# Attention of a two-block kernel: P turned in 32x32 blocks, P·V on row quarters, the output product in two halves

## What is computed

```python
qkv = h @ w_qkv                                   # 2048 x 2560: 2048 q, 256 k, 256 v
q, k = rope(rms_norm(q)), rope(rms_norm(k))       # per head of 64
scores = q . k / 8, only keys j with  i - 128 < j <= i
m = max(scores, sink);  p = exp(scores - m)
probs = p / (sum(p) + exp(sink - m))
out = probs @ v                                   # 256 x 2048
x = x + out @ w_o                                 # w_o is 2048 x 2048
x = x + (silu(h2 @ w_gate) * (h2 @ w_up)) @ w_down   # h2 = rms_norm(x)
```

## Time and profile before

| | |
|---|---|
| median of 3 runs | 1928.45 us |
| the profiled execution | 1928.84 us, span of the program in it 1927.0 us |
| PE (TensorE matmul) busy | 1920.7 us, 100% of the span |
| DVE (VectorE), ACT (ScalarE), POOL (GpSimd) busy | 1302.3, 1076.2, 556.6 us |
| granted TensorE clock | full in all 40 slices |
| DMA | 352 MB, 183 GB/s over the span, engines 50 to 90% busy |

### The profile page before, as it was taken

How to read it: one execution, slowest core, us unless ns; L and a number is a source line. 1 busy time by engine, 2 the same in 40 slices (tenths; PEclk the granted TensorE clock), 3 DMA queues, 4 the chain that set the end, 5 groups by cost and what they waited for, 6 DMA issues and landing times.

```text
span 1927.0 us, 26536 instructions
## 1 busy us (share of the span) xinstructions
PE 1920.7 (100%) x9696; PEld 1576.4 (82%) x9696; DVE 1302.3 (68%) x1852; ACT 1076.2 (56%) x1405; POOL 556.6 (29%) x616
## 2 busy tenths in 40 slices
PE   9999999999999999999999999999999999999999
PEld 7888878888888888888887778888888888888887
DVE  5899967546878888887667877555555555544443
ACT  7444466547768696875557775544444444443332
POOL 1899853306060413302401106022222222220000
PEclk9999999999999999999999999999999999999999
DMA  9665656566555555555564445666666666666664
GB/s 322 190 194 178 186 164 198 174 209 184 160 162 164 157 169 160 167 156 180 186 197 141 123 141 189 193 196 192 191 195 186 196 195 195 190 192 196 193 193 161
DMA packets 183152, 352.47 MB, mean 183 GB/s; under 512 B 11792, under 2 KB 12304, under 8 KB 183056
## 3 DMA queue, kind: packets, MB, share of 16 engines
q1 hardware_dynamic: 182912, 351.20, 59.7%
q10 hardware_dynamic: 144, 0.01, 0.0%
HBM read 349.07 MB, written 2.10 MB: 182 GB/s over the span
## 4 chain that ended last, share of the span: by engine, by line
PE 89%; DVE 3%; ACT 3%; POOL 2%; issue 1%; DVEq 1%; POOLq 0%; DMA 0%; ACTq 0%; SPq 0%
PE acc L550 28%; PE acc L552 28%; PE acc L551 28%; POOL kb L467 1%; PE T L660 1%; POOL kf L467 1%; DVEq L1175 1%; ACT E L1002 1%; PE T L509 1%; DVE w_lo L1189 1%; PE T L755 1%; PE T L744 1%; ACT w_hi L797 1%; DVE E L1416 0%; PE T L732 0%
## 5 line engine op out<-in xcount | busy, mean ns | idle before, releaser
L1189 DVE TENSOR_TENSOR w_lo<-raw,w_hi 128x1024 fp32r<-128x1024 f32 x568 | 699.1, 1234 | 533.9 <-ACT w_hi L797 526.1
L797 ACT ACTIVATE w_hi<-raw 128x1024 fp32r<-128x1024 f32 x656 | 688.7, 1057 | 594.7 <-PE acc L552 576.0
L550 PE MATMUL acc<-w_hi,h_hi 128*128 128x512 f32 x1884 | 741.7, 394 | 0.4 <-DVE w_lo L1189 0.2
L552 PE MATMUL acc<-w_hi,h_lo 128*128 128x512 f32 x1884 | 733.7, 389 | 0.0
L551 PE MATMUL acc<-w_lo,h_hi 128*128 128x512 f32 x1884 | 733.6, 389 | 0.0
L550 PEld LDWEIGHTS acc<-w_hi,h_hi 128*128 128x128 f32 x1884 | 353.7, 188 | 80.0 <-issue 5.1
L552 PEld LDWEIGHTS acc<-w_hi,h_lo 128*128 128x128 f32 x1884 | 353.6, 188 | 74.0
L551 PEld LDWEIGHTS acc<-w_lo,h_hi 128*128 128x128 f32 x1884 | 353.9, 188 | 71.2
L498 POOL COPY fT<-fq 32x256 f32<-32x256 f32 x176 | 110.9, 630 | 388.1 <-DVE fq L1651 381.3
L436 POOL TENSOR_TENSOR w_lo<-raw,w_hi 128x1024 fp32r<-128x1024 f32 x80 | 190.4, 2409 | 71.5 <-ACT w_hi L797 71.4
L1269 DVE SCALAR_TENSOR_TENSOR T<-vpad,feat,T 128x256 f32<-128x256 f32 x464 | 182.4, 476 | 0.0
(11 more groups left out here) (245 smaller groups left out, 1581.7 us busy)
## 6 DMA issues: line engine op xcount, KB each, us to landing
raw<-in_hgrn_w_in_dram SPq DMA_DIRECT2D x160, 512.0 KB, 3.7
raw<-in_conv_w_in_dram SPq DMA_DIRECT2D x96, 512.0 KB, 4.1
raw<-in_ffn_w_gate_dram SPq DMA_DIRECT2D x88, 512.0 KB, 4.4
raw<-in_ffn_w_up_dram SPq DMA_DIRECT2D x88, 512.0 KB, 4.2
raw<-in_ffn_w_down_dram SPq DMA_DIRECT2D x88, 512.0 KB, 4.8
raw<-in_attn_w_qkv_dram SPq DMA_DIRECT2D x40, 512.0 KB, 4.0
raw<-in_conv_w_out_dram SPq DMA_DIRECT2D x32, 512.0 KB, 4.6
raw<-in_hgrn_w_out_dram SPq DMA_DIRECT2D x32, 512.0 KB, 4.6
```

Source lines behind the costliest of these rows:

```text
L550: nc.tensor.matmul(o, hi[:, kt, a], w_hi[:, slot, kk, :], start=kt == 0, stop=False)
L552: last = nc.tensor.matmul(o, lo[:, kt, a], w_hi[:, slot, kk, :], start=False, stop=kt == p.chunks * CK - 1)
L797: A(w_hi[:, slot, :, :], raw[:, slot, :, :], ACT.Copy).then_inc(hi_ready, 1)
L1189: TT(w_lo[:, slot, :, :], raw[:, slot, :, :], rounded(w_hi[:, slot, :, :]), ALU.subtract).then_inc(split_ready, 1)
```

## The change

1. `low_by_pool`: GpSimd makes `w_lo` of three chunks in eight (i mod 8 = 7, 0, 1) in place of two.
2. P is no longer turned on TensorE. VectorE turns it in 32x32 blocks (`p_turn`, one instruction a head), which leaves block b of the keys of query quarter a on partitions 32a to 32a+31. `mix_v` now runs once a group, behind chunk e+16 (e+14 for g = 3): 60 matmuls of 32 rows by 64 columns by 128 streamed columns, each of the four row quarters into its own PSUM bank, two column halves side by side. V is spread to the four row quarters by GpSimd (`v_rows`), `PT` now holds eight heads and shares its place with `kvtok`.
3. `scale_p` moves from VectorE to GpSimd, two instructions for a pair of heads; VectorE keeps the reciprocal (`inverse`).
4. `y_out_hi` (ScalarE, e+20; e+18 for g = 3) and `y_low` (VectorE, e+21; e+18) take a whole group, four instructions each, 256 strided columns.
5. `att_out` becomes eight segments of four chunks: the four column groups over channels of heads 0 to 15, then again over the others. VectorE adds the first parts to `x` (`first_part`), four more times two additions. The interleaved start is gone.
6. Of x, two column groups (2 and 3) are turned on TensorE at the end of `att_out`, not one.

```diff
-    return 24 <= i < 50 and i % 8 < 2
+    return 23 <= i < 50 and i % 8 in (7, 0, 1)
...
+    def segment(self, k):
+        return k + self.columns if self.in_parts else k
+    def row(self, k, c):
+        return self.chunks * (k // self.columns) + c if self.in_parts else c
+    def first_reads(self, k):
+        return k == 0 or self.in_parts and k == self.columns
...
-            ... ("att_out", 1, 4, {"lead": 2}),
+            ... ("att_out", 1, 8, {"chunks": CPG // 2}),
...
+            def v_rows():
+                pool.wait_ge(a_ev, 1)
+                pool.wait_ge(a_T, 1)
+                for a in range(4):
+                    for b in range(4):
+                        nc.gpsimd.tensor_copy(vrows[a * QUARTER:(a + 1) * QUARTER, b::4, :], kvtok[b * QUARTER:(b + 1) * QUARTER, :, KVH * HD:])
+                nc.gpsimd.drain().then_inc(a_rows, 1)
+
+            def scale_p(g, i):
+                pool.wait_ge(a_inv, 4 * g + i + 1)
+                for tb in range(TB):
+                    p, inv = sm[:, 2 * i:2 * i + 2, (1 + tb) * P:2 * (1 + tb) * P], ast[:, 6, 8 * tb + 2 * i:8 * tb + 2 * i + 2]
+                    last = nc.gpsimd.tensor_tensor(p, p, inv.unsqueeze(2).to_broadcast([P, 2, (1 + tb) * P]), ALU.mult)
+                last.then_inc(a_n, 1)
...
+                    i = n - ph["kv_q"].chunk0
+                    if i % 8 == 1:
+                        for p in range(4):
+                            scale_p(i // 8 - 3, p)
...
-                    if need is not None and k == 0:
-                        need(c)
+                    row = p.row(k, c)
+                    if need is not None and p.first_reads(k):
+                        need(row)
...
             def q_turn(g):
                 pe.wait_ge(a_rp, g + 2)
                 pe.wait_ge(a_cp, 2)
                 if g:
-                    pe.wait_ge(a_ptc, 8 * g)
+                    pe.wait_ge(a_sm, 8 * g)
+                if g > 1:
+                    pe.wait_ge(a_lo, 4 * (g - 1))
                 transposes(T01, ar, a_T)
...
-            def turn_p(g, i):
-                ...
-                    for b in range(3):
-                        last = nc.tensor.transpose(T[:, h % 2, b * P:(b + 1) * P], sm[:, h, (b + 1) * P:(b + 2) * P], ident[:, :])
-            def mix_v(g, i):
-                ...
+            def mix_v(g):
+                pe.wait_ge(a_rows, 1)
+                pe.wait_ge(a_pt, 4 * g + 4)
+                pe.wait_ge(a_sm, 8 * (min(g + 1, 3) + 1))
+                if g:
+                    pe.wait_ge(a_lo, 4 * g)
                 for tb in range(TB):
+                    for step in range(5):
+                        for a in range(4):
+                            blocks = range(4 + a, 4 + a + 5) if tb else range(a + 1)
+                            if step >= len(blocks):
+                                continue
+                            b, r = blocks[step], slice(a * QUARTER, (a + 1) * QUARTER)
+                            key = b if b < 4 else b - 4
+                            for c in range(2):
+                                o = T[c * HD:(c + 1) * HD, a, :].rearrange("p (i t q) -> p i t q", t=TB, q=QUARTER)[:, 0:4, tb, :]
+                                w = PT[r, c:8:2, b * QUARTER:(b + 1) * QUARTER]
+                                last = nc.tensor.matmul(o, vrows[r, key, g * HD:(g + 1) * HD], w, start=step == 0, stop=step == len(blocks) - 1)
                 last.then_inc(a_o, 1)
...
-                for i in range(4):
-                    at.put(e + 8 + i, lambda g=g, i=i: turn_p(g, i))
-                    at.put(e + 9 + i, lambda g=g, i=i: mix_v(g, i))
+                at.put(e + 16 if g < 3 else e + 14, lambda g=g: mix_v(g))
...
-            stream("att_out", 0, y_hi, hy_lo, early, lambda c: pe.wait_ge(a_lo, c + 1))
+            stream("att_out", 0, y_hi, hy_lo, at.later(40).with_(last_x), lambda c: pe.wait_ge(a_lo, 2 * (c + 1)))
...
-            def p_copy(g, i):
-                ...
+            def y_out_hi(g):
+                act.wait_ge(a_o, g + 1)
+                for i in range(4):
+                    A(by_quarters(y_hi, 4 * g + i), mixed(i).rearrange("p a (b i) -> p a b i", b=TB), ACT.Copy).then_inc(a_hi, 1)
...
+                    at.put(e + 20 if g < 3 else e + 18, lambda g=g: y_out_hi(g))
...
+            def first_part(name, k):
+                dve.wait_ge(chunk_used, ph[name].done(0, k))
+                for tb in range(TB):
                     TT(x[:, tb, group_columns(k)], acc[:, ph[name].pair(k), tb, :], x[:, tb, group_columns(k)],
                        ALU.add).then_inc(pair_free[ph[name].pair(k)], 1)
...
+            def inverse(g, i):
                 dve.wait_ge(a_p, 4 * g + i + 1)
                 l, inv = ...
-                V.reciprocal(inv, l)
+                V.reciprocal(inv, l).then_inc(a_inv, 1)
+            def p_turn(g, i):
+                dve.wait_ge(a_n, 4 * g + i + 1)
+                ...
+                for h in (2 * i, 2 * i + 1):
+                    last = V.transpose(PT[:, h, :], sm[:, h, P:4 * P])
+                last.then_inc(a_pt, 1)
+            def y_low(g):
+                dve.wait_ge(a_hi, 4 * g + 4)
+                for i in range(4):
+                    low(by_quarters(hy_lo, 4 * g + i), mixed(i).rearrange("p a (b i) -> p a b i", b=TB), by_quarters(y_hi, 4 * g + i), a_lo)
...
+                    for i in range(4):
+                        at.put(e + 11 + i, lambda g=g, i=i: p_turn(g, i))
+                    at.put(e + 21 if g < 3 else e + 18, lambda g=g: y_low(g))
```

More of the change, by code:

```diff
@@ L114, in end @@
     def end(self, k):
-        return self.last[k] + 1
+        return self.last[self.segment(k)] + 1
 def phases():
@@ L122, in phases @@
             ("conv_ab", 4, 2, {}), ("conv_z", 1, 4, {}), ("conv_out", 1, 4, {}), ("hgrn", 4, 4, {}),
-            ("hgrn_z", 1, 4, {}), ("hgrn_out", 1, 4, {}), ("kv_q", 1, 5, {}), ("att_out", 1, 4, {"lead": 2}),
+            ("hgrn_z", 1, 4, {}), ("hgrn_out", 1, 4, {}), ("kv_q", 1, 5, {}), ("att_out", 1, 8, {"chunks": CPG // 2}),
             ("gate_up", FJ, 2, {}), ("down", 1, 4, {"chunks": FCH})):
@@ L442, in x_moves @@
             def x_moves(s):
-                for k in range(3):
+                for k in range(on_tensor(s)):
                     pool.wait_ge(n_q, 3 * (s - 1) + k + 1)
-                    if s == 3 and k == 2:
-                        pool.wait_ge(n_lo, 4 * (s - 1) + 1)
-                    elif s < 3 and k:
+                    if s < 3 and k:
                         pool.wait_ge(n_lo, 4 * (s - 1) + k)
@@ L547, in stream @@
                     for kk, tb in ((0, 0), (1, 0), (0, 1), (1, 1)) if ends else ((0, 0), (0, 1), (1, 0), (1, 1)):
-                        kt = c * CK + kk
+                        kt = row * CK + kk
                         o, a = acc[:, p.pair(k), tb, :], slice(tb * P, (tb + 1) * P)
-                        nc.tensor.matmul(o, hi[:, kt, a], w_hi[:, slot, kk, :], start=kt == 0, stop=False)
+                        nc.tensor.matmul(o, hi[:, kt, a], w_hi[:, slot, kk, :], start=c == 0 and kk == 0, stop=False)
                         nc.tensor.matmul(o, hi[:, kt, a], w_lo[:, slot, kk, :], start=False, stop=False)
                         last = nc.tensor.matmul(o, lo[:, kt, a], w_hi[:, slot, kk, :], start=False,
-                                                stop=kt == p.chunks * CK - 1)
+                                                stop=c == p.chunks - 1 and kk == CK - 1)
                         if ends and (kk, tb) == (1, 0):
@@ L563, in x_turn, with step @@
             def x_turn(name, s, free):
-                def step():
-                    pe.wait_ge(x_done, 4 * s)
+                def step(k):
+                    pe.wait_ge(x_done, 4 * (s - 1) + k + 1)
                     pe.wait_ge(*free)
-                    transposes(T01, x[:, :, group_columns(3)], n_T)
-                return Hooks().put(ph[name].end(3) + 2, step).later(32)
+                    transposes(T01 if k == 3 else T23, x[:, :, group_columns(k)], n_T)
+                at = Hooks()
+                for k in range(on_tensor(s), 4):
+                    at.put(ph[name].end(k) + 2, lambda k=k: step(k))
+                return at
             def normed(s):
@@ L842, in x_norm @@
                     e = ph[name].end(k)
-                    at.put(e + 3, lambda k=k: x_squares(s, k)).put(e + (4 if k == 3 else 8) + late(name, k), lambda k=k: x_hi(s, k))
+                    at.put(e + 3, lambda k=k: x_squares(s, k)).put(e + (4 if k >= on_tensor(s) else 8), lambda k=k: x_hi(s, k))
                 return at.put(ph[name].end(3) + 5, lambda: x_std(s))
@@ L1138, in _ @@
                         at.put(e + 9 + i, lambda g=g, i=i: exps(g, i))
-                    for i in range(4):
-                        at.put(e + 11 + i, lambda g=g, i=i: p_copy(g, i))
-                    for b in range(2):
-                        at.put(e + 13 + 2 * b, lambda g=g, b=b: y_out_hi(g, b))
```

(9 more changed lines are left out.)

100 lines of the change are left out of this document (40 added, 60 removed).

## The result

The changed kernel takes 1936.99 us (median of 5 runs, 1935.72 to 1938.28), the kernel before 1928.34 (5 runs of the same comparison): ratio 1.0046, 95% interval 1.0034 to 1.0057. It is slower by 0.5%, clear of the noise; 1930.2 was forecast, with a range up to 1936. The profiled execution took 1936.99 us, 8.15 more than the 1928.84 of before.

A forecast was written before the change was run, and what follows sets the result against it. TensorE was taken to bound every stretch. At the end, 2.7 us for the later q_turn(3), -1.9 for mix_v behind it and +0.9 for turning x made +1.7 on 1928.84 profiled; median forecast 1930.2 us, range 1924.5 to 1936.

The forecast's parts named there:

- What becomes late: Step following the ScalarE and VectorE chains: TensorE would wait 5.0, 5.8 and 7.1 us, and the end comes 1.7 later.
- Hidden: Work reckoned to cost nothing: GpSimd's spreading of V and third w_lo, more additions for x, the DMAs.
- TensorE's work: Step reckoning TensorE's load: 26.5 us removed, 9.6 for the new mix_v, 0.9 for turning x, net 16.0 less.
- C: Rival, chance 0.08: mix_v's tiles don't run eight at a time; 1932.8 us for four at a time, about 1962 for one.
- q_turn(1): First chain: it starts at 1052.4 after TensorE waits 5.0 us for rope, a gain of 1.7.
- q_turn(2): Second chain: 34.3 us after q_turn(1) against 32.74 before, TensorE waiting 5.8; the gain of 1.7 is eaten.
- dear copies: Case in which strided copies of y from PSUM take 0.8 us each instead of 0.39: about 1936 us.
- Chunk 42: Third chain, att_out reading y of group 1: TensorE waits 7.1 us, at least 3.0 however quick the rest.
- rival B: Chance 0.17: GpSimd's scale_p lengthens w_lo or rope on VectorE in three chains, +3.6 us, median 1933.8.
- Rival A: Chance 0.14: TensorE's saving comes through, every chain being 5 us shorter than reckoned; median 1915.5 us.

The follow-up runs named there:

- a_fill: The changed kernel with extra matmuls on TensorE in the waits before q_turn(1), q_turn(2) and chunk 42: 1931.03 us.
- b_held3: The kernel before, with q_turn(1) also waiting for three small DMAs one after the other: 1941.59 us.
- c_serial: The changed kernel with the matmuls of mix_v issued one row quarter after the other instead of step by step over the quarters: 1944.78 us.
- a_ylow: The changed kernel with y_low of groups 0 to 2 one chunk earlier on VectorE (e+20 instead of e+21): 1931.84 us.
- a_early: The changed kernel with four of GpSimd's 16 copies of V behind rope(0), y_low a chunk earlier, and q taken a chunk earlier: 1926.05 us.
- b_lead: a_early with w_lo of chunk 23 taken off GpSimd, att_out's start interleaved and y of group 1 read at chunk 44 instead of 42: 1923.40 us.
- b_best: b_lead with extra matmuls on TensorE in front of the waits of q_turn(1), (2) and (3): 1922.05 us.
- b_held1: The kernel before, with q_turn(1) also waiting for one small DMA issued when chunk 28 is done: median 1933.74 us.

## Why the prediction was wrong

The step that failed is "What becomes late". It found the waits (5.0, 5.8 and 7.1 forecast, 4.8, 4.8 and 6.7 measured, none before `q_turn(3)`) and priced each by its length alone. TensorE's work behind a wait was taken at the durations of a kernel that never waits, where the clock "is full in all of them". That was an extrapolation to a state which the trace of before does not contain. Missing is a term of 6.3 us, put at nothing: TensorE's low clock behind the waits. a_fill shows its size (6.0 us come back) and b_held3 that a wait alone brings it about. The second step that failed is in "Hidden": 1.2 us at `q_turn(0)`.

- TensorE's work: right. `mix_v` is 2.4 a group, as for eight tiles side by side; C falls. Its price was too low, though: a longer `mix_v` of groups 0 and 1 does not "cost nothing" (c_serial).
- `q_turn(1)`: right, 1053.05. Chunk 24 started 0.67 later than before, so 1052.4 becomes 1053.1.
- `q_turn(2)`: 36.0 us after `q_turn(1)`, 34.3 forecast. 2.4 are low clock. The strided y copies cost 0.26 to 0.33 each instead of 0.39, 0.8 less. The "dear copies" side of the range was empty.
- Chunk 42: the place and the wait were right. That it must cost 3.0 however quick the rest holds only for the order of steps in this kernel; a_ylow brings it to 0.3.
- "Hidden: GpSimd's spreading of V": wrong, 1.2 us. It was priced by GpSimd's free time and not by what VectorE does beside it. That is rival B's mechanism at a place that the prediction did not examine. Where B put it, beside `scale_p`, it costs nothing on the chains.
- Rival A: its condition, that every chain be shorter, was not met. a_early and b_lead show that the chains can be shortened by the order of steps, with chunk 23's w_lo back on VectorE: 5.5 us of the 16. With the waits filled (b_best) it is 6.8.
- The range: its upper end, 1936, had no case in which waits cost more than their length.

## What to carry to other kernels

When a change makes the busiest engine wait for the first time, its later work may not run at the speed that the old trace shows: price waits of some 2.6 us and more on TensorE with 1.4 to 2.8 us on top, as measured here in the traces where the clock fell (waits from 2.6 to 10.5 us), or with a range that starts at nothing for those near 3 us, and see whether the waits can be filled. Waits of 1.0 to 1.9 us left the clock at full. A helper engine's "free time" isn't free for its neighbour: write down what VectorE does in each stretch that GpSimd is given. And before a wait is accepted, see if it hangs on the order of steps alone: one number in a table (e+21 to e+20) was worth 5.2 us here, the low clock that it spared included.

## What was not expected of the hardware

- A wait of some 3.3 us before the same `q_turn(1)` costs only its length in some runs of b_held1 (1932.15 to 1932.54, mean clock 1.000) and up to 3 us more in others; in a_ylow 3.45 kept the clock and 3.17 lost it; in b_lead 2.6 lost it. What else decides it stays open.
- VectorE instructions of 8 columns can be held by GpSimd beside them as large ones are: 1.63 us for 0.17, and a copy of 8 columns at 1055.31 in the changed kernel took 1.48 for 0.11. Not every kind is held: the reductions just before the 1.63, beside the same work of GpSimd, took 0.69 and 1.22 as elsewhere.
- How far tiles on different row quarters run together depends on the order of issue: the same 120 records take 2.24 us step by step over the quarters and 4.29 quarter by quarter.
